# Storing the dense tokens' expert weights by groups of eight keys in a PEER encoder layer

## The reference

```python
v1, i1 = lax.top_k(s1, PEER_TOPK)
v2, i2 = lax.top_k(s2, PEER_TOPK)
cand = (v1[..., :, None] + v2[..., None, :]).reshape(nb, L, PEER_HEADS, PEER_TOPK * PEER_TOPK)
sc, ci = lax.top_k(cand, PEER_TOPK)
e = (jnp.take_along_axis(i1, ci // PEER_TOPK, axis=-1) * PEER_KEYS
     + jnp.take_along_axis(i2, ci % PEER_TOPK, axis=-1))
w = jax.nn.softmax(sc, axis=-1)
...
    act = jax.nn.gelu(jnp.einsum('td,tjd->tj', hx, u_tab[ex]), approximate=False)
    coef = (wx * act).astype(hx.dtype)
    return jnp.einsum('tj,tjd->td', coef, v_tab[ex])
```

## Time and profile before

| | us |
|---|---|
| median of 3 runs | 3138.53 |
| lowest and highest | 3136.22, 3140.13 |
| profiled execution, its own time | 3134.47 |
| its span | 3132.8 |
| TensorE busy | 2915.7 (93%) |
| VectorE busy | 2271.4 (73%) |
| GpSimd busy | 1243.1 (40%) |
| ScalarE busy | 843.3 (27%) |

### The profile page before, as it was taken

How to read it: one execution, slowest core, us unless ns; L and a number is a source line. 1 busy time by engine, 2 the same in 40 slices (tenths; PEclk the granted TensorE clock), 3 DMA queues, 4 the chain that set the end, 5 groups by cost and what they waited for, 6 DMA issues and landing times.

```text
span 3132.8 us, 31543 instructions
## 1 busy us (share of the span) xinstructions
PE 2915.7 (93%) x10300; PEld 1577.1 (50%) x10300; DVE 2271.4 (73%) x4447; ACT 843.3 (27%) x1692; POOL 1243.1 (40%) x1101
## 2 busy tenths in 40 slices
PE   7899989789789999799999999996999999999995
PEld 3455777667575444344445454453444444444442
DVE  4798355550677799999788888885676766766777
ACT  3112443321221101465466566680000000000003
POOL 0111111012225544444344434445544565655652
PEclk9999899889889999899999999998999999999998
DMA  4541110023238999999999999999999999999995
GB/s 178 181 158 70 55 41 28 21 81 128 81 101 346 413 413 386 333 394 367 345 359 366 339 361 339 412 416 405 404 403 406 399 406 402 401 399 402 401 399 203
DMA packets 287037, 919.80 MB, mean 294 GB/s; under 512 B 26016, under 2 KB 75424, under 8 KB 279456
## 3 DMA queue, kind: packets, MB, share of 16 engines
q0 software_dynamic: 147456, 536.94, 44.0%
q1 hardware_dynamic: 100784, 301.75, 25.4%
q10 hardware_dynamic: 38640, 79.18, 6.6%
HBM read 830.21 MB, written 87.56 MB: 293 GB/s over the span
## 4 chain that ended last, share of the span: by engine, by line
PE 27%; DMA 23%; DVE 8%; POOL 7%; issue 3%; ACT 1%; SPq 1%; DVEq 0%; ACTq 0%; POOLq 0%
PE s_pu L1587 21%; DMA s_slot<-in_v,s_row 17%; POOL s_slot L1542 7%; DMA s_slot<-in_u,s_row 5%; DVE s_slot L1995 4%; PE s_pw L1624 3%; PE s_py L1634 2%; DVE s_hB L2009 2%; DMA s_wr<-s_w 1%; SPq L1506 1%; DMA s_w<-s_wb 0%; SPq L1500 0%; ACT y L1843 0%; ACT s_hotw L1763 0%; PE s_py L1685 0%
## 5 line engine op out<-in xcount | busy, mean ns | idle before, releaser
L1587 PE MATMUL s_pu<-s_hn,s_ut 128*128 128x512 f32 x2304 | 1012.0, 595 | 6.0 <-ACT s_gst L1710 4.7
L2009 DVE SCALAR_TENSOR_TENSOR s_hB<-s_slot,s_dot,s_hB 128x1024 f32<-128x1024 f32 x469 | 597.4, 1284 | 273.5 <-DMA s_slot<-in_v,s_row 271.1
L1542 POOL DMA_INDIRECT s_slot<-in_v,s_row x512 | 593.1, 1158 | 434.0 <-DVE s_hB L2009 328.3
L1542 POOL DMA_INDIRECT s_slot<-in_u,s_row x512 | 501.7, 980 | 640.6 <-DVE s_slot L1995 555.8
L1587 PEld LDWEIGHTS s_pu<-s_hn,s_ut 128*128 128x128 f32 x2304 | 434.4, 191 | 532.7 <-issue 530.1
L1995 DVE SCALAR_TENSOR_TENSOR s_slot<-s_slot,s_ph 128x1024 f32<-128x1024 f32 x512 | 610.1, 1219 | 80.0 <-DMA s_slot<-in_u,s_row 60.9
L1763 ACT ACTIVATE s_hotw<-s_hot,s_rest 128x128 bf16<-128x128 bf16 x1024 | 308.5, 423 | 52.4 <-ACT s_gst L1710 25.5
L1668 PE MATMUL s_pw<-s_ct,s_vt 128*128 128x512 f32 x512 | 249.9, 612 | 42.2 <-DMA s_vt<-in_v_tiles 42.2
L1820 ACT ACTIVATE s_sq<-y 128x512 f32<-128x512 f32 x16 | 8.9, 628 | 944.7 <-DVE y L2058 944.7
L311 PE MATMUL s_ps<-hn_hi,w_hi 128*128 128x512 f32 x576 | 238.7, 414 | 21.2 <-POOL w_lo L299 11.8
L1668 PE MATMUL s_pu<-s_ct,s_vt 128*128 128x512 f32 x512 | 245.3, 602 | 0.0
(11 more groups left out here) (293 smaller groups left out, 3138.2 us busy)
## 6 DMA issues: line engine op xcount, KB each, us to landing
s_ut<-in_u_tiles SPq DMA_DIRECT2D x128, 512.0 KB, 7.2
s_vt<-in_v_tiles SPq DMA_DIRECT2D x32, 2048.0 KB, 20.6
s_g<-s_gst ACTq DMA_DIRECT2D x128, 256.0 KB, 7.0
s_w<-s_wb ACTq DMA_DIRECT2D x16, 2048.0 KB, 11.3
s_gr<-s_g SPq DMA_DIRECT2D x64, 512.0 KB, 27.5
s_wr<-s_w SPq DMA_DIRECT2D x16, 2048.0 KB, 30.0
s_ada<-in_ada SPq DMA_DIRECT2D x48, 512.0 KB, 5.6
s_ada<-in_ada SPq DMA_DIRECT2D x4, 2048.0 KB, 20.2
```

The lines of the kernel that those rows point to most:

```text
L1542: pool.indirect_dma_start(out=slot[s][:, :], out_offset=None, in_=io[kind], in_offset=bass.IndirectOffsetOnAxis(ap=row[b][:, j:j + 1], axi ...
L1587: mm = pe.matmul(pu[:, n % 2, :], ut[n % UR][:, k, :], hn[:, k, :], start=(k == 0), stop=(k == DC - 1))
L2009: dve.scalar_tensor_tensor(y, s, dot[b][:, j:j + 1], y, ALU.mult, ALU.add).then_inc(taken, 1)
```

## The change

The tensor in DRAM is laid out by groups of eight keys, `[group, partition, chunk x key x token]`. The load of a group takes from each partition one run of 16 KB. The store of a chunk writes for each partition 16 runs of 1 KB, one for each group; the groups lie 2 MB apart, the partitions 16 KB. The buffers on the chip, the order of all instructions, the semaphores and the bytes moved stay as they are.

```diff
-WT = 32
+WT, WG = 32, 8
...
-    WG = 8
...
-        w4 = m.w.rearrange("c p (k t) -> p c k t", t=WT)
...
-                sp.dma_start(wr[g % 2][:, :, :, :], w4[:, :, WG * g:WG * g + WG, :]).then_inc(w_in[g % 2], 16)
+                sp.dma_start(wr[g % 2][:, :, :, :].rearrange("p c k t -> p (c k t)"), m.w[g]).then_inc(w_in[g % 2], 16)
...
-                    act.dma_start(m.w[chunk], wb[chunk % 2][:, :, :].rearrange("p k t -> p (k t)"))\
+                    act.dma_start(m.w[:, :, WG * WT * chunk:WG * WT * (chunk + 1)].rearrange("g p x -> p g x"),
+                                  wb[chunk % 2][:, :, :].rearrange("p (g k) t -> p g (k t)", k=WG))\
                        .then_inc(w_stored[chunk % 2], 16)
...
-    m.w = dram("s_w", [HALF // WT, P, KEYS * WT])
+    m.w = dram("s_w", [KEYS // WG, P, WG * HALF])
```

## The result

The changed kernel takes 3187.84 us in the median of four runs (3169.62 to 3192.75), the kernel before beside it 3137.38 (3133.89 to 3140.13). The ratio is 1.0156, 95% interval 1.0132 to 1.0179: 50 us slower. The forecast said slower at 3222, range 3150 to 3300. The direction held and so did the mechanism in the main; the loss is 57% of the 88 us forecast. The runs of the changed kernel spread over 23 us, those before over 6.

The account below looks back on a forecast made before the run. Stage A was taken as bound by TensorE with ScalarE close behind, stage B by the DMA engines with TensorE close behind. Terms: +108 (A) + 0 (passage) - 20 (B) = +88 on 3134.5, giving 3222 us, range 3150 to 3300.

Parts of the forecast that it names:

- Price of the runs: Weight stores in stage A: 2 MB in 1 KB runs lands 30 us after issue, ends 22 and 36.
- the second rival: Stage A: same mechanism at half strength, landings 22 to 25 us, +35 to +60, total 3150 to 3175; chance 0.14.
- The hold: ScalarE's next g store issue is held until 12 us after the weight store, ends 0 and 20.
- Late A: Three late weight stores in stage A: hold plus wait for landing cost 14.4 us each, 43 in all.
- Middle A: Nine stores with gaps between batches: 5 us each in the mean, 45 in all, landing waits hidden.
- The blocks' ends: Three stores ending token blocks in stage A: hold hidden, Gelu's landing wait costs 5 us each, 15 in all.
- The clock: Stage A: TensorE runs slower for some microseconds after a stall; +5, most starts beside a ScalarE late anyway.
- The passage: From stage A to B: later landing of the last store offset by faster first loads; zero, -5 to +15.
- Stage B: Long-run weight loads let the full DMA engines move more and remove v stalls: -20, ends 0 and -31.
- The first: ScalarE neither held nor short of landings, since VectorE paces the gathers in stage A: 3118; chance 0.14.
- The third: Stores dearer than loads, writing runs 2 MB apart: +6 landing, +3 hold, stage A some +200, total 3315; chance 0.07.
- The fourth: Run length does not matter for stores or loads: time unchanged, 3135 us; chance 0.04.

Follow-up runs that it names:

- both_short: Changed kernel's 1 KB-run store combined with the 1 KB-run load of the kernel before (output of other products); 3212.9 us, ratio 1.0238.
- three_gst: Changed kernel with three buffers for the Gelu's output in place of two; 3181.33 us, ratio 1.0153.
- the four kernels of store and load: Weight store and load each in 16 KB or 1 KB runs, in all pairings, the kernel before and the changed one included; 3115.51 to 3212.9 us.
- both_long: Kernel before's 16 KB-run store combined with the changed kernel's 16 KB-run load (output of other products); 3115.51 us, ratio 0.9936.
- at_once: Changed kernel with each weight store cut into four DMAs of 512 runs, issued one right behind the other; 3202.03 us, ratio 1.0214.
- quarters: Changed kernel with each weight store cut into four DMAs of 512 runs, issued one per tile from ScalarE; 3119.34 us, ratio 0.9951; again 3121.69, 0.9957.

## Why the prediction was right, and where its sizes were off

"Late" are the thirteenth to fifteenth store, "block ends" the fourth, eighth and twelfth, "middle" the other nine of the first twelve; the sixteenth is in the passage.

- **Price of the runs.** Right in kind, too high in size. The price seen on SP's loads did go to ScalarE's stores, but the 30 us were taken from stage B, where even a v tile in 16 KB runs takes 18.2. In stage A the short-run stores land after 21.5 us in the median in both_short and 22.8 in three_gst, which are the second rival's 22. The g stores queued behind them landed 34.9 and 31.2 us after the weight stores of 1990.91 and 2202.34, as the 32 forecast; at the five earlier stores where a Gelu waited for one, it was 30.0, 25.0, 25.4, 21.5 and 24.7 us. Behind the three late stores the Gelu ran at 29.7, 24.4 and 26.0 us without waiting for a landing.
- **The hold.** Right that ScalarE would be held at its next g store; mis-sized. I let every queue be free 12 us after the weight store. The late holds end 13.1, 7.3 and 9.9 us after it, that of the sixteenth store 13.6, those of the middle between 4 and 14. The example with its long gap (1384.99) was not held at all: by 7.6 us its queue was free.
- **Late A.** Forecast 43 us of idle time, measured 21.8 (10.26, 4.46 and 7.04). This term was off most. The forecast let the landing add 4.3 us to each hold, and it added none. The holds cost 7.3 us each in the mean, not 10.1.
- **Middle A.** Forecast 45, measured 26.4, from six of the nine stores. The landing was not hidden everywhere: behind the first store the Gelu waited 11.89 us for it and TensorE idled 6.94.
- **The blocks' ends.** Forecast 15, measured 12.6, all of it at the third. The waits of ScalarE for landings at the first two (9.4 and 11.0 us) did not reach TensorE.
- **Together.** These three make the 61 us of new idle time for the 103 forecast. With the slower matmuls behind the stalls the weight stores come later than before by 32 us over the late ones, 41 over the middle and 11 over the blocks' ends (1.3 us were there before the first store, and 3.5 are back by the end of A). I had said that each store would be later against before than the one ahead of it: the fifth, seventh and ninth are not.
- **The clock.** Forecast +5, measured +20 (878.21 for 857.93 us of the same matmuls). The reason I gave, that ScalarE is late anyway and hides it, was wrong: at a stall of 4.46 us TensorE lost 1.2 us in the placing and 1.5 in the next tile, on the path. It made up for 15 of the 42 us by which the idle time was forecast too high, which is luck. Stage A: forecast +108, measured +81.5.
- **The passage.** 0 forecast, +0.8 measured, and for the reason given: the weight load waits 18 us longer for the last store, and the long-run loads behind it save 21 (17.8 us for 38.4; 20 were forecast). The last store also lies 3.5 us closer to the end of A.
- **Stage B.** -20 forecast, -25 measured; by the four kernels of store and load, 18 of it are from the loads and 6 from gathers that had caught up while TensorE stood still, which I had not counted.
- **Rivals.** The first is refuted by the holds. Its argument, that the gathers' issuer mostly waits for VectorE, may be why the landings in A are short of 30 us; no run separates this. The second had the landings right and the time wrong: its 3150 to 3175 had too little for holds and clock. The third, dearer writes at 2 MB steps, has no sign: in both_short the stores land after 21.5 us and the loads after 29.4. The fourth (run length without effect) is refuted by both effects in the four kernels of store and load.

## What to carry to other kernels

When a layout moves short runs from loads to stores, ask whose queue takes them and what that engine must do next. 2048 runs at once held their issuer for up to 14.2 us here (in both_short); on an engine without reserve this was the step's critical path, on SP with three tiles in hand it cost a sixth (13.6 us of stage A for 81.5). Cut into four parts and spaced over four tiles the same runs cost nearly nothing (1 to 5 us of stage A), and only then did the layout bring its gain. Take a price from the stage in which it will be paid: in both_short 2 MB in 1 KB runs took 21.5 us as a store in stage A and 29.4 as a load in stage B. Where two waits on one engine have one cause, ask what the second adds to the first, and add what TensorE loses by its clock after each stall.

## What the runs showed that was not expected

- The backlog is about spacing alone: four DMAs of 512 runs cost 3202 us issued at once and 3119 issued one per tile.
- Where the DMA engines are full, a longer passage can be given back: 39.0 us of it in both_long, with a stage B of 888 us behind it. A v tile loaded early only changed who was waited for.
- The kernels with backlogs are mostly less steady: the four runs of the changed one span 23 us, of at_once 19 and of both_short 18, those of quarters 5, and 8 the second time. three_gst, with backlogs too, spans 5, so backlogs alone do not make it.
